# Output product by halves of a tile, feed-forward and router starts reordered, small fetches moved, in a two-layer decoder trunk

## The reference, cut to what matters

```python
for layer in range(DEPTH):                       # DEPTH = 2
    h = rms_norm(x, norm1[layer])
    proj = h @ w_in[layer]                       # q, three k/v pairs, gates, convolution
    ...
    mixed = jnp.concatenate([rms_norm(o_attn, attn_out_norm[layer]),
                             rms_norm(o_conv, conv_out_norm[layer])], axis=-1)
    x = x + mixed @ w_out[layer]                 # the output product
    h = rms_norm(x, norm2[layer])
    if layer % 2 == 0:
        x = x + swiglu(h, ffn_w_gate[i], ffn_w_up[i], ffn_w_down[i])
    else:
        x = x + moe_swiglu(h, router_w[i], router_b[i], moe_w_gate[i], moe_w_up[i], moe_w_down[i])
# moe_swiglu: logits = h @ router_w + router_b; the two largest of eight; sort, gather, products, scatter
```

## Time and profile before

| | us |
|---|---|
| median of three runs | 2253.69 |
| lowest and highest run | 2250.65, 2256.49 |
| profiled execution, its own time | 2255.06 |
| its span | 2253.2 |
| TensorE busy (share of the span) | 2145.5 (95%) |
| VectorE busy | 555.4 (25%) |
| ScalarE busy | 286.4 (13%) |
| POOL busy | 70.5 (3%) |

### The profile page before, as it was taken

How to read it: one execution, slowest core, us unless ns; L and a number is a source line. 1 busy time by engine, 2 the same in 40 slices (tenths; PEclk the granted TensorE clock), 3 DMA queues, 4 the chain that set the end, 5 groups by cost and what they waited for, 6 DMA issues and landing times.

```text
span 2253.2 us, 31239 instructions
## 1 busy us (share of the span) xinstructions
PE 2145.5 (95%) x13342; PEld 1707.2 (76%) x13342; DVE 555.4 (25%) x1343; ACT 286.4 (13%) x769; POOL 70.5 (3%) x77
## 2 busy tenths in 40 slices
PE   7999997999999999999859999999999999999994
PEld 3554545888864446445549999999999999999993
DVE  2245634332344212564220010010101001010102
ACT  1133311111100112332000000000000000000000
POOL 2100000000000010000000000000000000000001
PEclk9999998999999999999859999999999999999997
DMA  8111012232230330100076667778787777878743
GB/s 321 65 38 38 14 66 112 75 112 75 89 154 0 149 142 38 38 1 1 38 287 236 228 223 267 263 269 296 266 290 267 285 287 292 296 289 309 287 160 121
DMA packets 41913, 382.39 MB, mean 170 GB/s; under 512 B 5138, under 2 KB 5170, under 8 KB 14768
## 3 DMA queue, kind: packets, MB, share of 16 engines
q1 hardware_dynamic: 34192, 355.68, 42.3%
q0 software_dynamic: 4704, 14.40, 2.0%
q10 hardware_dynamic: 2880, 10.32, 1.1%
HBM read 367.94 MB, written 14.54 MB: 170 GB/s over the span
## 4 chain that ended last, share of the span: by engine, by line
PE 93%; DVE 3%; DMA 2%; issue 1%; ACT 1%; POOL 0%; ACTq 0%; DVEq 0%; POOLq 0%
PE ps L421 30%; PE ps L430 15%; PE ps L1078 12%; PE ps L908 8%; PE ps L1094 6%; PE ps L845 6%; PE ps L1016 5%; PE ps L971 2%; PE ps L946 2%; PE ps L959 2%; PE ps L851 1%; PE ps L921 1%; PE ps L402 1%; PE ps L378 1%; DMA hT<-expert_rows,iw 1%
## 5 line engine op out<-in xcount | busy, mean ns | idle before, releaser
L421 PE MATMUL ps<-work,arena 128*128 128x136 f32 (+3 forms) x5632 | 704.0, 283 | 0.7 <-issue 0.7
L421 PEld LDWEIGHTS ps<-work,arena 128*128 128x128 f32 x5632 | 686.0, 191 | 1.2 <-issue 0.8
L430 PE MATMUL ps<-hid,arena 128*128 128x136 f32 (+3 forms) x2816 | 364.7, 283 | 0.0
L430 PEld LDWEIGHTS ps<-hid,arena 128*128 128x128 f32 x2816 | 348.4, 191 | 0.2 <-issue 0.2
L591 DVE TENSOR_TENSOR hid<-sg,ps 128x136 f32<-128x136 f32 (+3 forms) x176 | 52.7, 299 | 899.4 <-ACT sg L692 898.8
L908 PE MATMUL ps<-hT,arena 128*128 128x512 f32 x384 | 206.8, 638 | 0.0
L692 ACT ACTIVATE sg<-ps 128x136 f32<-128x136 f32 (+3 forms) x176 | 50.6, 287 | 927.4 <-PE ps L421 927.4
L1078 PE MATMUL ps<-hT,arena 128*128 128x256 f32 x704 | 160.6, 387 | 4.7 <-ACT arena L1734 3.0
L1078 PEld LDWEIGHTS ps<-hT,arena 128*128 128x128 f32 x704 | 136.9, 195 | 24.8 <-ACT arena L1734 3.4
L845 PE MATMUL ps<-arena,hT 128*128 128x512 f32 (+1 forms) x384 | 130.3, 497 | 0.0
L1078 PE MATMUL ps<-work,arena 128*128 128x256 f32 x528 | 119.3, 383 | 2.2 <-DVE work L1453 2.2
(11 more groups left out here) (236 smaller groups left out, 1289.0 us busy)
## 6 DMA issues: line engine op xcount, KB each, us to landing
arena<-m_w SPq DMA_DIRECT2D x176, 1536.0 KB, 6.6
arena<-f_gu SPq DMA_DIRECT2D x11, 2048.0 KB, 8.1
arena<-w_cv SPq DMA_DIRECT2D x8, 1536.0 KB, 23.9
arena<-w_o SPq DMA_DIRECT2D x4, 2048.0 KB, 7.6
arena<-f_dn SPq DMA_DIRECT2D x4, 2048.0 KB, 7.9
arena<-w_q SPq DMA_DIRECT2D x2, 2048.0 KB, 11.5
arena<-w_kv SPq DMA_DIRECT2D x2, 2048.0 KB, 13.6
arena<-bias_by_query_and_key SPq DMA_DIRECT2D x2, 2048.0 KB, 8.8
```

The costliest lines, as they stand in the source:

```text
L421: m = mm(ps[:, s % 2, j * CAP:j * CAP + W], w[:, k, :], xT[:, k, 0:W], start=(k == 0), stop=(k == KD - 1))
L430: m = mm(ps[:, 2 + j // 2, (j % 2) * CAP:(j % 2) * CAP + W], down_w[s % NSLOT][:, j * P:(j + 1) * P], hid[:, s % 2, 0:W], start=(s == 0 an ...
```

## The change

**Output product.** It now uses banks 0 to 3 alone (bank = 2 x part + half) and signals by half tiles: part 0 and part 1 of one half, a step of `po_ps`, VectorE's two adds, a step of `xres`, for which the same half of the next tile waits. A tile's norm work follows its second half directly, and its turn stands after the first half of the next tile, in banks 4 to 7. The output rows of `moe_loads` are stored as they come.

**Feed-forward start.** Pair 0 begins with a wait for all eight half tiles and goes products 1, 2, turn of tile 3, product 1 of pair 1, then 5, 6, 3, 7; pair 1 leaves its product 1 out. The zero rows are issued in pair 4.

**Router.** Its products of tiles 0 to 2 stand ahead of tile 3's turn, in bank 4. Its two fetches are issued by POOL in layer 0.

**Start.** Constants and first gain are issued by ScalarE, the bias table's products stand between turns 1 and 2, VectorE's copies of them behind norm 0.

The diff, without the lines that only rename, renumber a bank or move a function's body:

```diff
--- before
+++ after
@@ -354,3 +354,2 @@
         def moe_loads(sp):
-            sp.wait_ge(po_ps, TT * DEPTH)
             for t in range(TT):
...
@@ -365,2 +364,3 @@
 
+            sp.wait_ge(po_ps, 2 * TT * DEPTH)
             sp.wait_ge(meta_done, 1)
...
@@ -372,8 +372,12 @@
 
-        def moe_products(pe):
+        def moe_products(pe, norm_turn, turned):
 
             pe.wait_ge(router_in, 32)
+            turned(3, 2)
             for t in range(TT):
+                if t == TT - 1:
+                    norm_turn(3, t)
+                    turned(3, t)
                 for k in range(KD):
-                    m = mm(ps[:, 0, E * t:E * (t + 1)], hT[:, k, t * P:(t + 1) * P], rw[:, k, :], start=(k == 0), stop=(k == KD - 1))
+                    m = mm(ps[:, 4, E * t:E * (t + 1)], hT[:, k, t * P:(t + 1) * P], rw[:, k, :], start=(k == 0), stop=(k == KD - 1))
             m.then_inc(rl_ps, 1)
...
@@ -736,5 +740,2 @@
         def moe_gathers(pool):
-            pool.dma_start(rw[:, :, :], r_w).then_inc(router_in, 16)
-            pool.dma_start(rb, r_b.to_broadcast([P, E])).then_inc(router_in, 16)
-
             def gather(W):
...
@@ -831,7 +832,8 @@
 
-            pe.wait_ge(table_in, 32)
...
+            def bias_by_distance():
+                pe.wait_ge(table_in, 32)
+                pe.wait_ge(zeroed, 1)
+                for i in range(2):
+                    m = mm(ps[0:H, 2 + i, 0:320], table_sb[0:33, :], oh_sb[0:33, i * 320:(i + 1) * 320], start=True, stop=True)
+                m.then_inc(bias_ps, 1)
 
...
@@ -840,2 +842,4 @@
                     for t in range(TT):
+                        if t == 2:
+                            bias_by_distance()
                         norm_turn(0, t)
...
@@ -855,5 +859,5 @@
                 pe.wait_ge(wq_in, 16 * (L + 1))
-                if L == 0:
-                    pe.wait_ge(bias_sb, 1)
                 for t in range(TT):
+                    if L == 0 and t == 2:
+                        pe.wait_ge(bias_sb, 1)
                     turned(2 * L, t)
...
@@ -1011,7 +1015,5 @@
 
-                def out_products(t, j, ks):
-                    part, hf = j // 2, j % 2
-                    m = None
+                def out_products(t, part, hf, ks):
                     for k in ks:
-                        m = mm(ps[:, 4 * (t % 2) + j, :], mixT[:, 4 * part + k, t * P:(t + 1) * P],
+                        m = mm(ps[:, 2 * part + hf, :], mixT[:, 4 * part + k, t * P:(t + 1) * P],
                                WO[part][:, k, hf * 512:(hf + 1) * 512], start=(k == 0), stop=(k == 3))
...
@@ -1050,24 +1052,19 @@
 
-                for t in range(TT):
-                    if t == 0:
-                        pe.wait_ge(wo_in[1], 16 * (L + 1))
-                        pe.wait_ge(cvm_done, CT * (L + 1))
-                        pe.wait_ge(ptd, NP * (L + 1))
-                        pe.wait_ge(pta, NP * (L + 1))
-                    if t == 1:
-                        pe.wait_ge(osq_done, TT * (L + 1))
-                        pe.wait_ge(totals_read, L + 1)
-                        pe.wait_ge(mix_done, TT * (L + 1))
-                    if t >= 2:
-                        pe.wait_ge(xres, TT * L + t - 1)
-                    for j in range(4):
-                        m = out_products(t, j, (2, 3) if t == 0 and j == 1 else range(4) if t or j else ())
-                        if t == 0 and j == 2:
-                            o_total(TT - 1)
-                            conv_totals()
-                    m.then_inc(po_ps, 1)
-                if L:
-                    for t in range(TT):
-                        norm_turn(3, t)
-                    turned(3, TT - 1)
+                pe.wait_ge(wo_in[1], 16 * (L + 1))
+                pe.wait_ge(cvm_done, CT * (L + 1))
+                pe.wait_ge(ptd, NP * (L + 1))
+                pe.wait_ge(pta, NP * (L + 1))
+                out_products(0, 1, 0, range(4)).then_inc(po_ps, 1)
+                o_total(TT - 1)
+                conv_totals()
+                out_products(0, 0, 1, (2, 3))
+                out_products(0, 1, 1, range(4)).then_inc(po_ps, 1)
+                for t in range(1, TT):
+                    pe.wait_ge(mix_done, TT * L + t + 1)
+                    for hf in range(2):
+                        pe.wait_ge(xres, 2 * (TT * L + t - 1) + hf + 1)
+                        out_products(t, 0, hf, range(4))
+                        out_products(t, 1, hf, range(4)).then_inc(po_ps, 1)
+                        if hf == 0:
+                            norm_turn(2 * L + 1, t - 1)
 
...
@@ -1098,5 +1095,4 @@
 
-                norm_turn(1, 0)
-                norm_turn(1, 1)
                 turned(1, 1)
+                pe.wait_ge(xres, 2 * TT)
                 for j in range(NPAIR):
...
@@ -1106,8 +1102,6 @@
                         pe.wait_ge(hid1_done, j - 1)
-                    product(1, j % 2, raw[:, :, 0, :], h11, True)
+                    if j != 1:
+                        product(1, j % 2, raw[:, :, 0, :], h11, True)
                     if j:
                         last_product(j - 1)
-                    else:
-                        norm_turn(1, 2)
-                    if j:
                         pe.wait_ge(c_done, 3 * j - 3 + C11)
...
@@ -1116,3 +1110,5 @@
                         norm_turn(1, 3)
-                    else:
+                        pe.wait_ge(raw_in[1], 16)
+                        product(1, 1, raw_w[1][:, :, 0, :], h11, True)
+                    if j:
                         pe.wait_ge(c_done, 3 * j - 3 + C12)
...
@@ -1196,9 +1192,13 @@
             dve.wait_ge(const_in, 16)
-            dve.wait_ge(bias_ps, 1)
...
+            def bias_rows():
+                dve.wait_ge(bias_ps, 1)
+                for i in range(2):
+                    m = v.tensor_copy(bias_row[:, 320 * i:320 * (i + 1)], ps[0:H, 2 + i, 0:320])
+                m.then_inc(bias_sb, 1)
 
             def norm(ns, before=None):
-                dve.wait_ge(gain_in, 16 * (ns + 1))
+                if ns:
+                    dve.wait_ge(gain_in, 16 * ns)
+                else:
+                    dve.wait_ge(gain0_in, 16)
                 for t in range(TT):
...
@@ -1242,2 +1245,3 @@
                     norm(0)
+                    bias_rows()
                 else:
...
@@ -1439,11 +1443,13 @@
                 v.sem_inc(totals_read, 1)
+                dve.wait_ge(gain_in, 16 * (2 * L + 1))
                 for t in range(TT):
-                    dve.wait_ge(po_ps, TT * L + t + 1)
-                    for j in range(4):
-                        xs = x[:, t, (j % 2) * 512:(j % 2 + 1) * 512]
-                        m = v.scalar_tensor_tensor(xs, ps[:, 4 * (t % 2) + j, :], rac[:, TT * (j // 2) + t:TT * (j // 2) + t + 1], xs, ALU.mult, ALU.add)
-                        if j == 1:
-                            after(m)
-                    m.then_inc(xres, 1)
-                norm(2 * L + 1)
+                    for hf in range(2):
+                        dve.wait_ge(po_ps, 2 * (TT * L + t) + hf + 1)
+                        xs = x[:, t, hf * 512:(hf + 1) * 512]
+                        after(v.scalar_tensor_tensor(xs, ps[:, hf, :], rac[:, t:t + 1], xs, ALU.mult, ALU.add))
+                        v.scalar_tensor_tensor(xs, ps[:, 2 + hf, :], rac[:, TT + t:TT + t + 1], xs, ALU.mult, ALU.add).then_inc(xres, 1)
+                        if hf == 0 and t:
+                            norm_copy(2 * L + 1, t - 1)
+                    norm_tile(2 * L + 1, t)
+                norm_copy(2 * L + 1, TT - 1)
 
...
@@ -1560,4 +1566,9 @@
         def _(se):
+            se.dma_start(cst[:, :], const).then_inc(const_in, 16)
+            se.dma_start(gb[:, :], n_b[0:1, :].to_broadcast([P, D])).then_inc(gain0_in, 16)
+
             def norm(ns):
                 for t in range(TT):
+                    if ns % 2 and t:
+                        norm_copy(ns, t - 1)
                     if ns == 0:
...
@@ -1567,3 +1578,3 @@
                     else:
-                        se.wait_ge(xres, TT * (ns // 2) + t + 1)
+                        se.wait_ge(xres, 2 * (TT * (ns // 2) + t + 1))
                     if ns or t:
...
@@ -1571,3 +1582,3 @@
                     act(junk, x[:, t, :], ACT.Square, accum_out=ss[:, t:t + 1]).then_inc(ss_done, 1)
-                    if t >= 1:
+                    if ns % 2 == 0 and t:
                         norm_copy(ns, t - 1)
...
@@ -1728,3 +1739,3 @@
                         silu_of_last(j - 1)
-                    else:
+                    if j == 4:
                         se.wait_ge(zeroed, 2)
...
@@ -1747,6 +1758,4 @@
         def _(pool):
-            pool.dma_start(cst[:, :], const).then_inc(const_in, 16)
             pool.dma_start(table_sb[0:32, :], table).then_inc(table_in, 16)
             pool.dma_start(oh_sb[0:33, :], onehot).then_inc(table_in, 16)
-            pool.dma_start(gb[:, :], n_b[0:1, :].to_broadcast([P, D])).then_inc(gain_in, 16)
```

(2 more changed lines are left out.)

33 lines of the change are left out of this document (14 added, 19 removed).

## The result

The changed kernel takes 2221.31 us (median of 4 runs, 2219.85 to 2222.36) against 2253.97 for the kernel before, run beside it: a ratio of 0.9857, 95% interval [0.9844, 0.9869]. The profiled execution took 2222.33 (span 2220.5), 32.7 less than the 2255.06 (2253.2) of before. Forecast were 2217 and a saving of 37.4.

A forecast was written before the change was run, and what follows sets the result against it. TensorE, 93% of the chain of waits, was taken to bound the kernel, with gains only where it idles or clocks low. Gains 4.2 + 18.2 + 15.0 = 37.4 from 2255.06 gave 2217.7, stated as 2217; range 2213 to 2228.

The forecast's parts named there:

- Start: Kernel start: earlier gain and constants, norm ahead of table copies; query products near 19.3 instead of 23.5, gain 4.2 us.
- Like the x tiles, 5.7, so 7.0: At the start, the gain from ScalarE's queue takes 5.7 us like the equally large x tiles, landing at 7.0.
- The bound from the gain's own row: At the start, the gain stays as slow from issue as before, 8.6 us, landing at 9.9; gain 2.0 us.
- The fetch rival: At the start, x, weights and gain divide the same transfers: 2.0 us instead of 4.2, time 2219 to 2220; chance 0.18.
- Output product of layer 0: Three turns fit among its products, adding 2.7 us; only tile 1 waits, 0.4 us for the norm factors.
- Feed-forward start: From layer 0's output product to pair 0's product 4: 30.6 us with turns and lost wait, against 48.8; gain 18.2.
- Router: After layer 1's output product: 24 products fill the wait, router done in 11.5 us; gain 15.0, between 13.4 and 17.8.
- slow end: Router stage if the clock falls 3.8 us after the output product: 13.0 us instead of 11.5.
- Clock rival: Clock falls in the short feed-forward pauses and early under the router products: gain 29.6 us, time 2225; chance 0.18.
- Turns lowering the clock: Turns amid output products leave each tile's rest at half rate: 74 us over both layers, time 2291; chance 0.03.
- Covered later: The removed stalls were hidden by something later, for instance expert weights; 2237 if 20 us were eaten; chance 0.04.

The follow-up runs named there:

- weights_after_gain: The changed kernel, but SyncE issues the query weights and all later ones only when the gain has landed: 2218.87 us (1 run).
- gain_behind_x0: The changed kernel, but SyncE issues gain and constants directly behind the first tile of x: 2219.36 us.
- zeros_in_pair0: The changed kernel, but ScalarE issues the seven zero-row transfers in pair 0 again instead of pair 4: 2226.86 us.
- pair1_in_place: The changed kernel, but product 1 of pair 1 stands in pair 1 again: 2225.00 us.
- router_last: The changed kernel, but all 32 router products stand behind the turn of tile 3: 2229.89 us.
- after_again: The changed kernel itself, unchanged, run once more beside the last three kernels: 2221.02 us.

## Why the prediction was nearly right

The time lay in the range, 4.3 above the forecast. By its own steps:

- **Start: the mis-sized term.** "Like the x tiles, 5.7, so 7.0" failed. The x tiles' 5.7 was measured while SyncE's queue had most of the rate for itself, 1.16 of the 1.54 MB moved from 3 to 7 us; the move itself brought constants and gain to the front, SyncE's share fell to 0.85 of 1.58 MB, and x went to 8.5, the gain to 9.2. Worth 1.5 (21.96 against 23.50), not 4.2. The bound from the gain's own row, 8.6 and so 9.9, was the nearest, if still 0.4 too early. The row was also misread: 8.6 is the middle of two loads, and the first, which counts, took 8.0 and landed at 11.0, not at 11.7. The fetch rival put the start at 2.0 and the time at 2219 to 2220 and was nearer. Of its reason the weights fell (weights_after_gain), while x and the gain do share the transfers. The Trainium skill, "DMA: Bandwidth & Descriptors", section "Issuing engines are not separate DMA queues", says that another issuer saves only the issue time; the trace agrees for the gain, issued 1.9 earlier and landed 0.7 earlier. Queue and place matter all the same (5.0 in gain_behind_x0).
- **Output product of layer 0: right.** Three turns, no idle before them, clock 1.00. Tile 1's wait was 0.77, forecast 0.4.
- **Feed-forward start: right in each part.** Pause 1.83 (1.5), no wait before the sums' products, a hole of 0.83 (0.95), product 4 after 27.9 (27.5); the zero rows' issues are worth 5.6 (zeros_in_pair0), product 1 of pair 1 3.1 (pair1_in_place). To compare the whole stage, take the last point at which the order is the same, 116 records before the output product's end, in the kernel before:

```profile
298.67 5.42 PE L1016 MATMUL ps<-arena 128*128 128x512 f32 x12
```

and after:

```profile
297.42 3.70 PE L1018 MATMUL ps<-arena 128*128 128x512 f32 x8
```

  The lead there is 1.25; at product 4 of pair 0 (398.60 before) it is 18.44. So the stage gave 17.2 of the 18.2. The three pauses, 0.6 longer in sum than forecast, are part of the difference; the other 0.4 was not traced.
- **Router: right, with some luck.** 14.65 of 15.0; 11.9 against 11.5. The same code took 11.2 to 14.2 in the executions of the table, twice more than the 13.0 that the prediction took as its slow end (13.3 and 14.2). Its mechanism, products filling the wait before the clock falls, is shown by router_last (21.6).
- **Clock rival: false in the changed kernel.** The pauses of 0.83 and 1.83 did not lower the clock, and under the router's products it held for 4.9 us. In weights_after_gain and after_again it fell earlier there. In other kernels a pause of 2.21 behind a turn lowered it (pair1_in_place), and one of 3.69 too.
- **Turns lowering the clock: false here.** 1.00 in the 45 us with turns among products. "TensorE: Matmul & The Clock Gate" of the Trainium skill, "Part 4: PE-mode transpose", says that transposes don't count as busy in the same way; nothing of it shows where 1.04 us of them stand between 7 us of products, and the start of router_last, at the end of this document, speaks against it.
- **Covered later: false.** The lead is 18.3 at layer 1's output product, taken at the same point as the 1.25, and 32.8 at the first expert product.

The sum: 1.25 + 17.2 + 14.65 = 33.1 against 32.7 measured. Its first term is not the start's 1.5 brought through. The lead was 1.5 at the first query product and 2.8 at the gate products (95.62 against 92.83), since the clock rose earlier in this execution, and 1.25 only behind an attention that took 1.5 longer (208.1 against 206.6). Both are differences of the clock in the same code, so that they nearly cancel is luck. The forecast range mixes two bases as well: 2253.69 - 25.4 gives the 2228, 2255.06 - 42.4 the 2213.

## What to carry to other kernels

A landing time read from a trace belongs to the load of that moment: if a change moves several fetches to the front, add up the bytes that will be under way together and count with the slowest row, not with that of the nearest kind. A row that stands for several loads is a median: look up the one that is meant. Where an engine hands over to a stage that needs its last tile normed, find work that needs only the earlier tiles and put it in the gap; size it to the latency (here 4.9 us), and look for the small hole that opens where that work stood. Judge edits of a few microseconds by the stage that they touch, since other stages differ by as much from one execution to the next.
